# Second one-hot and its gate products stored token by token, first one-hot used as made, without GpSimd's copy of it

## The reference, cut to what matters

```python
def peer_ffn(x, w_q, sub_keys, u_tab, v_tab):       # 128 x 128 = 16384 experts, D = 1024
    q = (xb @ w_q).reshape(PEER_BLOCK, PEER_HEADS, 2, PEER_D_KEY // 2)
    s = jnp.einsum('thcd,cnd->thcn', q, sub_keys)
    s1, i1 = lax.top_k(s[:, :, 0], PEER_TOPK)
    s2, i2 = lax.top_k(s[:, :, 1], PEER_TOPK)
    ...
    experts = jnp.take_along_axis(cand_e, top_pos, axis=-1)    # i1 * 128 + i2
    gate = jax.nn.softmax(top_s, axis=-1)
    act = jax.nn.gelu(jnp.einsum('thkd,td->thk', u_tab[experts], xb))
    return jnp.einsum('thk,thkd->td', gate * act, v_tab[experts])
```

## Time and profile before

| | |
|---|---|
| three runs, median (lowest to highest) | 3269.68 us (3267.78 to 3274.24) |
| the profiled execution's own time | 3266.96 us |
| its span | 3265.2 us |
| PE busy | 2851.1 us, 87% |
| DVE busy | 1882.5 us, 58% |
| ACT busy | 1119.7 us, 34% |
| POOL busy | 282.0 us, 9% |
| mean granted TensorE clock | 0.924 |

### The profile page before, as it was taken

The page is one execution under the profiler, slowest core; times in us unless marked ns, Lnnn a source line. Parts: engine busy times, 40 slices in busy tenths (PEclk is TensorE's granted clock), DMA queues, the critical chain, the costliest instruction groups (busy, mean ns, idle before and its releaser), DMA issues.

```text
span 3265.2 us, 60101 instructions
## 1 busy us (share of the span) xinstructions
PE 2851.1 (87%) x22131; PEld 2596.3 (80%) x22131; DVE 1882.5 (58%) x3520; ACT 1119.7 (34%) x2050; POOL 282.0 (9%) x377
## 2 busy tenths in 40 slices
PE   6845667999999999997569999976799999999998
PEld 5634555899999999996348888861589999999998
DVE  2265553698889655541533444452169888955554
ACT  1222210244444444441123444430024444444443
POOL 0013210000111000000001111112000011100000
PEclk9968977999999999998768999996799999999999
DMA  4300001354444455554001222225245444445554
GB/s 151 116 18 21 15 9 55 119 181 153 143 143 147 156 180 180 181 188 167 0 1 41 58 58 58 58 62 150 83 131 181 149 145 145 143 162 181 181 181 139
DMA packets 112351, 377.98 MB, mean 116 GB/s; under 512 B 14569, under 2 KB 24042, under 8 KB 111538
## 3 DMA queue, kind: packets, MB, share of 16 engines
q1 hardware_dynamic: 88562, 322.17, 29.5%
q0 software_dynamic: 13248, 43.98, 4.5%
q10 hardware_dynamic: 10368, 9.44, 1.0%
HBM read 371.52 MB, written 4.01 MB: 115 GB/s over the span
## 4 chain that ended last, share of the span: by engine, by line
PE 71%; issue 15%; DVE 9%; ACT 2%; DMA 1%; ACTq 1%; DVEq 0%; SPq 0%; POOLq 0%; POOL 0%
PE ps L709 69%; DVE arena L1215 3%; ACT arena L1836 2%; DVE arena L1219 1%; DMA arena<-in_cache_n 1%; PE ps L959 1%; PE ps L746 1%; DVE arena L1599 1%; DVE arena L1590 1%; ACTq L529 1%; DVE arena L1229 0%; ACTq L530 0%; DVE ring_lo L1215 0%; DVE arena L1594 0%; PE ps L965 0%
## 5 line engine op out<-in xcount | busy, mean ns | idle before, releaser
L1215 DVE TENSOR_TENSOR ring_lo<-ring,w_hi 128x1024 fp32r<-128x1024 f32 x512 | 625.8, 1225 | 457.5 <-ACT w_hi L1836 451.7
L1836 ACT ACTIVATE arena<-ps 128x264 f32<-128x264 f32 (+18 forms) x1021 | 413.7, 424 | 1249.9 <-PE ps L709 1083.6
L709 PE MATMUL ps<-arena 64*64 64x64 f32 (+11 forms) x5228 | 570.1, 297 | 187.2 <-DVEq L1212 62.2
L709 PEld LDWEIGHTS ps<-arena 64*64 64x64 f32 (+6 forms) x5228 | 444.0, 166 | 303.6 <-issue 74.2
L1836 ACT ACTIVATE w_hi<-ring 128x1024 fp32r<-128x1024 f32 x512 | 541.8, 1059 | 390.6 <-PE ps L709 390.2
L709 PE MATMUL ps<-x_hi,w_hi 128*128 128x264 f32 x2048 | 595.0, 291 | 15.5 <-DVE ring_lo L1215 15.5
L709 PE MATMUL ps<-h_hi,w_hi 128*128 128x264 f32 x2048 | 580.1, 283 | 6.8 <-DVE ring_lo L1215 6.8
L709 PE MATMUL ps<-x_lo,w_hi 128*128 128x264 f32 x2048 | 584.9, 286 | 0.0
L709 PE MATMUL ps<-x_hi,ring_lo 128*128 128x264 f32 x2048 | 583.8, 285 | 0.0
L709 PE MATMUL ps<-h_lo,w_hi 128*128 128x264 f32 x2048 | 582.3, 284 | 0.0
L709 PE MATMUL ps<-h_hi,ring_lo 128*128 128x264 f32 x2048 | 582.1, 284 | 0.0
(11 more groups left out here) (164 smaller groups left out, 2281.2 us busy)
## 6 DMA issues: line engine op xcount, KB each, us to landing
ring<-in_wstream SPq DMA_DIRECT2D x608, 512.0 KB, 3.3
arena<-in_cache_t POOLq DMA_DIRECT2D x128, 192.0 KB, 2.6
arena<-in_cache_n ACTq DMA_DIRECT2D x72, 128.0 KB, 2.7
arena<-in_cache_n POOLq DMA_DIRECT2D x56, 128.0 KB, 2.8
arena<-in_mla_w POOLq DMA_DIRECT2D x1, 3072.0 KB, 10.2
arena<-in_state POOLq DMA_DIRECT2D x4, 512.0 KB, 4.2
out_wkv_s<-arena POOLq DMA_DIRECT2D x4, 512.0 KB, 3.9
arena<-in_consts SPq DMA_DIRECT2D x1, 1408.0 KB
```

The costliest lines, as they stand in the source:

```text
L709: return nc.tensor.matmul(out, lhsT, rhs, start=start, stop=stop, **kw)
L1215: return v.tensor_tensor(out, a, b, op)
L1836: return nc.scalar.activation(out, in_, func, **kw)
```

## The change

- `oh2` is stored (u n), token by token: the output is 512 adjacent elements; `keys8` is read with a step of 4 elements (8 bytes), and the index of the token is broadcast along the innermost dimension (step 0).
- `oh2g` is stored (k u n): output and `oh2` are read and written with step 1, the gate is broadcast along the innermost dimension (step 0).
- `oh1` is made as before; PE reads it directly as weights, with a step of 4 elements. The moving operand `oh2g[st][:, k, u, :]` is now 128 adjacent elements.
- GpSimd's `gate_rows`, its 132 copies, the buffer `oh1c` and the semaphores `oh1_ready` and `oh1_made` are gone. The place of `keys8` in the arena stays.

```diff
-        oh_words = OHT * 5 * P // 2
+        oh_words = OHT * 4 * P // 2
...
-        oh2 = [a[:, OHT * P:2 * OHT * P].rearrange("p (n u) -> p n u", u=OHT) for a in oh]
-        oh1c = [a[:, 2 * OHT * P:3 * OHT * P].rearrange("p (u n) -> p u n", u=OHT) for a in oh]
-        oh2g = [a[:, 3 * OHT * P:].rearrange("p (k n u) -> p k n u", k=2, u=OHT) for a in oh]
+        oh2 = [a[:, OHT * P:2 * OHT * P].rearrange("p (u n) -> p u n", u=OHT) for a in oh]
+        oh2g = [a[:, 2 * OHT * P:].rearrange("p (k u n) -> p k u n", k=2, u=OHT) for a in oh]
...
-            def gate_rows(layer):
-
-                for i in range(NSETS):
-                    pool.wait_ge(oh1_made, NSETS * layer + i + 1)
-                    nc.gpsimd.tensor_copy(oh1c[i % OHS], oh1[i % OHS].rearrange("p n u -> p u n")).then_inc(oh1_ready, 1)
...
-                    pe.wait_ge(oh1_ready, s0 + i + 1)
                     pe.wait_ge(oh2g_made, s0 + i + 1)
                     for u in range(OHT):
                         for k in range(2):
-                            last = mm(ps[:, b, u * P:(u + 1) * P], oh1c[st][:, u, :], oh2g[st][:, k, :, u], k == 0, k == 1)
+                            last = mm(ps[:, b, u * P:(u + 1) * P], oh1[st][:, :, u], oh2g[st][:, k, u, :], k == 0, k == 1)
...
-                    tt(oh1[st], keys8, these(0, 1).broadcast_to([P, P, OHT]), ALU.is_equal).then_inc(oh1_made, 1)
-                    tt(oh2[st], keys8, these(1, 1).broadcast_to([P, P, OHT]), ALU.is_equal).then_inc(oh2_made, 1)
+                    tt(oh1[st], keys8, these(0, 1).broadcast_to([P, P, OHT]), ALU.is_equal)
+                    tt(oh2[st], keys8.rearrange("p n u -> p u n"),
+                       idxh[:, 1, i * OHT:(i + 1) * OHT].unsqueeze(2).broadcast_to([P, OHT, P]), ALU.is_equal).then_inc(oh2_made, 1)
                     dve.wait_ge(oh2_made, s0 + i + 1)
-                    tt(oh2g[st], oh2[st].unsqueeze(1).broadcast_to([P, 2, P, OHT]),
-                       these(2, 2).unsqueeze(2).broadcast_to([P, 2, P, OHT]), ALU.mult).then_inc(oh2g_made, 1)
+                    wide = [P, 2, OHT, P]
+                    tt(oh2g[st], oh2[st].unsqueeze(1).broadcast_to(wide),
+                       these(2, 2).unsqueeze(3).broadcast_to(wide), ALU.mult).then_inc(oh2g_made, 1)
```

More of the change, by code:

```diff
@@ L472, in build @@
         sel_ready = sem("sel_ready")
-        oh1_ready = sem("oh1_ready")
         oh_used = sem("oh_used")
-        oh1_made = sem("oh1_made")
         oh2_made = sem("oh2_made")
@@ L655, in _ @@
             pool.wait_ge(st_out, 64)
-            gate_rows(0)
             pool.wait_ge(x_added, 2)
@@ L681, in _ @@
                     page(pool, cache_n, it * NSLOT + n, cpN[n], natp_in[n])
-            gate_rows(1)
             pool.wait_ge(x_added, 4)
```

## The result

| | before | after |
|---|---|---|
| median of 8 runs each | 3271.96 us | 3253.41 us |
| lowest to highest | 3266.6 to 3281.35 | 3249.94 to 3259.69 |
| the profiled execution, its span | 3266.96, 3265.2 | 3255.23, 3253.5 |
| one layer's eleven periods, first gate set to last | 277.87 us | 268.96 us |

The ratio is 0.9943, 95% interval 0.9926 to 0.9959: faster by 0.57%, some 18.6 us, where 3270 us and no change were forecast.

A forecast was written before the change was run, and what follows sets the result against it. PE was taken to bound every period, with DVE nearly full. PE's faster sets and DVE's slower operations (+481 ns a set) cancel to +0.5 us, against the median 3270.2 rounded to 3270 us; range 3243 to 3313.

The forecast's parts named there:

- What bounds the stage: Eleven periods per layer: PE busy for all 25.87 us before; after, DVE exceeds that in the last five, PE's sets unchanged.
- `oh2` 691 ns and `oh2g` 1225: DVE's two one-hot operations drop to one element per cycle: +275 and +206 ns, together +481 ns a set.
- Rival 1: Strided reads cost DVE's oh2 the step-16 reduction's price, 1013 ns: +41 us, 3311 us; chance 0.21.
- rival 2: DVE keeps two elements per cycle for oh2g (675 ns) and never fills: 3240 us; chance 0.17.
- One reason given for 691: For oh2 on DVE: GpSimd's copy, same 8-byte steps, took 698 to 796 ns for 512 elements, near one per cycle.
- the prediction's own line: DVE operations at one element per cycle: 1.04 ns an element plus some 158 ns fixed, so 691 ns for 512.
- the bound for DVE: DVE's time per period: busy time, plus 2.89 us from slower one-hots, plus 0.38 us gaps; 27.40 us in the tenth.
- PE's sets: PE's eight f16 matmuls per gate set: 87 ns each, the middle between 58 and 116; -0.23 us a set, period 24.47 us.
- The prediction's own table: Period by period, the longer of PE and DVE, plus the closing part: +0.3 us a layer, +0.5 us for both.
- off the path: GpSimd's 777 ns copy: PE never waits for it; removing it would gain oh2g up to 344 ns at its old rate.
- The closing wait: The 3.42 us wait ahead of the output tiles, forecast to stay about as it is.
- mine: DVE at one element per cycle, no strided price: 3270 us, own range 3263 to 3281; chance 0.52.

The follow-up runs named there:

- e2: Changed kernel with the gate multiplied into the first one-hot (stepped weights), the plain second one-hot as packed moving operand: 3221.91 us, ratio 0.9857 to before.
- e6: Changed kernel with the second one-hot made twice, one more 688 ns DVE operation per set: 3332.49 us, ratio 1.0175 to before.
- e3: Changed kernel with oh2 number-major as before; only the product oh2g is turned, reading oh2 with 8-byte steps: 3231.24 us, ratio 0.9894 to before.
- e1: Kernel before with only GpSimd's copy removed; PE reads weights and moving operand with steps of 4 elements: 3280.28 us, ratio 1.0035 to before.
- e5: Changed kernel with GpSimd's copy of the first one-hot and PE's wait for it put back: 3297.87 us, ratio 1.0076 to before.
- e4: Changed kernel with oh2 and oh2g stored as pairs of tokens, product in two instructions, moving operand stepping 4 bytes: 3224.23 us, ratio 0.9871 to before.
- e7: Changed kernel with the gate in the first one-hot, stored as token pairs (weights step 4 bytes), second one-hot packed: 3221.51 us, ratio 0.9835 to before.

## Why the prediction was wrong, point by point

- **What bounds the stage**, PE before and DVE in the late periods after: right, and shown by e2 and e6. DVE set it from the fourth period on.
- **`oh2` 691 ns and `oh2g` 1225**: measured 688 and 1225. Rival 1 (strided reads as in the step-16 reduction, 1013 ns) and rival 2 (pairing kept) are both out. With 8-byte steps DVE pays for the lost pairing and nothing more (e3 as well), which agrees with the Trainium skill, "SBUF — State Buffer", on cachelines; TensorE's moving operand does not follow that note, as the same 8-byte step costs it 54 ns a matmul (e1 against e2). The Trainium skill's page "VectorE: DVE Perf Modes", Mode 2×_1P, which asks for a step of ±1 on reads too, agrees with both durations. One reason given for 691 was right by luck: GpSimd's copy was no measure of a stepped read, since by e5's reading some 0.27 us of its 777 ns was waiting for DVE. And two per cycle for 1024 elements is 691 ns by the prediction's own line, not 675; e1 measured 692.
- **The step that failed is the bound for DVE, "its busy time + 2.89 + 0.38"**, 27.40 us in the tenth period, which took 26.44. The 2.89 us hold: 0.46 to 0.48 us a set are 2.8 to 2.9. What they were added to does not. I read the late periods as operations that "stand end to end", with one wait and 0.38 us of gaps. In fact `ring_lo` waited for ACT in all seven tiles of a period, and while it is held it cannot overlap the operation ahead of it (1040.01 + 1.80 against its start at 1041.85, in the tenth period). With nothing to wait for, it starts 0.08 us before that one ends (1059.17 + 2.28 against 1061.37). Seven of these overlaps give a full DVE back 0.57 us a period, and it is idle 0.21 us, not 0.38: 24.13 + 2.89 - 0.57 + 0.21 = 26.66 us. The 0.66 us wait in the first set would have told.
- **PE's sets**: 0.70 us forecast from the middle of two bounds; by the same formula, (23.58 - 7 x 2.90) / 6, they take 0.55, or 68 ns a matmul, below the middle taken (87). This is the second term that was mis-sized. The stepped moving operand was nearly the whole cause of the 116 ns, and stepped weights cost little.
- **What each term was worth.** The prediction's own table, both layers: +0.5 us as forecast. With PE's 0.55 alone it gives -0.1, since DVE's bound keeps it from counting. With DVE's bound put right alone, -11.6. With both, -15.2; measured periods, -17.8. The rest fits DVE's lead, which the table did not carry over. Its three operations for the set that opens PE's tenth period began 7.0 us ahead of that set before, and 4.6 after. The second and third periods stayed at 23.58 us although their work exceeds that, 1.7 us for both layers. The late periods are about 0.2 us each under the table's, 3.0 in all, and the closing part is 1.05 us over in each layer, with six `ring_lo` in it in place of five. That the lead accounts for all of it is not shown.
- **The copy**: "off the path" was true of the kernel before and of what PE waited for, and rightly priced in `oh2g`. That its cover is gone once DVE is full, I did not say; e5 puts it at 44 us.
- **The closing wait** ahead of the output tiles stayed, as forecast: 3.4 us once in the stage of layer 0.

With mine as the likeliest case, its own range began at 3263 us, allowing for 0.1 us less in DVE's two operations. PE's short sets and DVE's lower bound come together at the low end, and make each other count: two uncertain terms under a maximum are not a sum. That 3253 us still lies between 3243 and 3313 is luck: that end was held for rival 2, which did not occur.

The version to keep is e2, 3221.91 us, 1.4% below before: the same products, no GpSimd in the stage, and the gate multiplied into the operand that may be stepped.

## What to carry to other kernels

When one engine's gain is capped by another's load, find how much work the second has when nothing holds it, from distances between starts in a stretch without waits. Its busy time plus its small gaps overstates that, as an operation that waits also loses its overlap with the one ahead. An added instruction costs its distance between starts (0.60 us for one of 0.69, e6); one made longer costs the growth of its duration. Then take both terms to their bounds together before calling it a draw. Ask for each operand which engine minds its step: here an f16 moving operand of TensorE minds 8 bytes, weights hardly, and VectorE minds any break in the pairs, so the gate belongs in the stepped weights and the plain one-hot in the moving operand. A copy that hides under one bound is not free under the next; test removals singly and together.

## What the runs showed of the hardware that I had not expected

- Moving operand, 128 f16 columns: period with a step of 2 bytes 23.58 us, 4 bytes 23.70, 8 bytes 26.16 (e2, e4, e1; weights with 8-byte steps in all three; 48 matmuls each). 2.5 ns a matmul at 4 bytes, 54 ns at 8.
- Weights with 8-byte steps cost 0.29 us a period against packed ones (e1 against before), beside a moving operand with 8-byte steps; beside a packed one, 0.15 us less with 4-byte steps than with 8 (e7 against e2).
- The runs fit VectorE and GpSimd excluding each other by whole instructions: a copy of 777 ns grows to 1047 behind an `oh2` that is 272 ns longer, and `oh2g` grows by 330 ns behind the copy whether it takes 692 ns or 1225 by itself.
- In e6, PE was idle for 4.4 of the 30.05 us of the tenth period, and the granted clock was 0.94 there; in e5, idle for 4.4 of 28.41 us, it was 1.00. What made the difference no run here shows.
